# A two-layer PEER and attention stack on one core: the first two output chunks of three projections taken together, and the first picks turned one or two steps sooner

## The reference, cut to what matters

```python
def conformer_conv(h, w1, b1, ...):
    u = h @ w1 + b1                       # 1024 -> 2048: "conv_in"
    a, g = jnp.split(u, 2, axis=-1)
    u = a * jax.nn.sigmoid(g)
    ...
def peer(h, wq, sk1, sk2, u_tab, v_tab):  # once in each of the two layers
    q = (xc @ wq).reshape(PEER_CHUNK, PEER_HEADS, 2, PEER_HALF)   # 1024 -> 2048: "peer_query"
    s1 = jnp.einsum('chd,kd->chk', q[:, :, 0], sk1)
    s2 = jnp.einsum('chd,kd->chk', q[:, :, 1], sk2)
    v1, i1 = lax.top_k(s1, PEER_TOPK); v2, i2 = lax.top_k(s2, PEER_TOPK)
    ...                                   # the 16 best pairs of keys, softmax over their scores
    act = jax.nn.gelu(jnp.einsum('cd,chkd->chk', xc, u), approximate=False)
    return jnp.einsum('chk,chkd->cd', gate * act, v)
```

## Time and profile before

| | us |
|---|---|
| median of 3 runs | 2810.82 (2805.54 to 2812.44) |
| the profiled execution, its own time | 2802.38 |
| its span | 2800.6 |
| TensorE matmul busy | 2706.8 (97%) |
| VectorE busy | 2033.5 (73%) |
| ScalarE busy | 1510.7 (54%) |
| GpSimd busy | 615.6 (22%) |

### The profile page before, as it was taken

The page is one execution under the profiler, slowest core; times in us unless marked ns, Lnnn a source line. Parts: engine busy times, 40 slices in busy tenths (PEclk is TensorE's granted clock), DMA queues, the critical chain, the costliest instruction groups (busy, mean ns, idle before and its releaser), DMA issues.

```text
span 2800.6 us, 60626 instructions
## 1 busy us (share of the span) xinstructions
PE 2706.8 (97%) x21599; PEld 2607.8 (93%) x21599; DVE 2033.5 (73%) x4480; ACT 1510.7 (54%) x3277; POOL 615.6 (22%) x659
## 2 busy tenths in 40 slices
PE   9999999999999998999999999999998899998998
PEld 8899889999999997889899999999987799987998
DVE  7759988787787865779888777777676665556665
ACT  7453355555555554652455555555545655556554
POOL 1033680021111213125850010010044300022000
PEclk9999999999999999999999999999999999999999
DMA  5055427787887843256347677676643046532564
GB/s 182 7 168 175 128 74 248 228 293 248 266 269 245 291 146 117 64 167 201 99 139 233 223 238 237 224 239 221 188 136 125 21 155 186 180 126 78 159 194 135
DMA packets 153654, 493.92 MB, mean 176 GB/s; under 512 B 18033, under 2 KB 37937, under 8 KB 153489
## 3 DMA queue, kind: packets, MB, share of 16 engines
q1 hardware_dynamic: 137424, 437.67, 48.0%
q0 software_dynamic: 15488, 54.11, 6.8%
q10 hardware_dynamic: 576, 0.03, 0.0%
HBM read 481.62 MB, written 10.13 MB: 176 GB/s over the span
## 4 chain that ended last, share of the span: by engine, by line
PE 87%; DVE 8%; ACT 2%; issue 1%; POOL 1%; DMA 0%; POOLq 0%; DVEq 0%; ACTq 0%
PE banks L841 67%; PE banks L1085 7%; PE banks L1244 2%; PE banks L1106 2%; PE banks L983 2%; DVE meta_row L2343 1%; DVE work L2346 1%; PE banks L879 1%; PE banks L874 1%; POOL x_lo L2841 1%; DVE w_lo L545 1%; ACT w_hi L538 1%; DVE arena L2326 1%; PE banks L1361 0%; DVE att_small L2633 0%
## 5 line engine op out<-in xcount | busy, mean ns | idle before, releaser
L545 DVE TENSOR_TENSOR w_lo<-ring,w_hi 128x512 fp32r<-128x512 f32 x1448 | 1014.0, 704 | 551.2 <-ACT w_hi L538 527.2
L538 ACT ACTIVATE w_hi<-ring 128x512 fp32r<-128x512 f32 x1448 | 908.9, 630 | 756.0 <-PE banks L841 710.2
L841 PE MATMUL banks<-gated_all,w_hi 128*128 128x240 f32 (+1 forms) x5120 | 886.2, 278 | 6.4 <-DVE gated_all L2410 6.4
L841 PE MATMUL banks<-x_hi,w_hi 128*128 128x240 f32 (+2 forms) x3008 | 853.2, 284 | 22.5 <-POOL x_lo L2841 7.2
L841 PE MATMUL banks<-x_lo,w_hi 128*128 128x240 f32 (+2 forms) x3008 | 843.7, 280 | 0.0
L841 PE MATMUL banks<-x_hi,w_lo 128*128 128x240 f32 (+2 forms) x3008 | 839.2, 279 | 0.0
L841 PEld LDWEIGHTS banks<-gated_all,w_hi 128*128 128x128 f32 x5120 | 776.5, 190 | 8.3 <-DVE gated_all L2410 8.3
L841 PE MATMUL banks<-gated_all,w_lo 128*128 128x240 f32 (+1 forms) x2560 | 706.9, 276 | 0.0
L841 PEld LDWEIGHTS banks<-x_hi,w_hi 128*128 128x128 f32 x3008 | 572.6, 190 | 36.0 <-issue 13.9
L841 PEld LDWEIGHTS banks<-x_hi,w_lo 128*128 128x128 f32 x3008 | 574.0, 191 | 0.0
L841 PEld LDWEIGHTS banks<-x_lo,w_hi 128*128 128x128 f32 x3008 | 572.4, 190 | 0.5
(11 more groups left out here) (369 smaller groups left out, 2835.2 us busy)
## 6 DMA issues: line engine op xcount, KB each, us to landing
ring<-in_peer_v SPq DMA_DIRECT2D x256, 512.0 KB, 3.6
ring<-in_peer_u SPq DMA_DIRECT2D x184, 512.0 KB, 4.5
arena<-in_peer_u SPq DMA_DIRECT2D x72, 512.0 KB, 3.7
ring<-in_mlp_up SPq DMA_DIRECT2D x64, 512.0 KB, 3.5
ring<-in_mlp_down SPq DMA_DIRECT2D x64, 512.0 KB, 3.5
ring<-w_peer_query SPq DMA_DIRECT2D x32, 512.0 KB, 3.5
ring<-w_fox_proj SPq DMA_DIRECT2D x24, 512.0 KB, 3.5
ring<-w_nsa_proj SPq DMA_DIRECT2D x20, 512.0 KB, 3.5
```

The source lines that it names most:

```text
L538: act.activation(w_hi[:, hn % SPLITS], raw_half(hn), ACT.Copy).then_inc(hi_ready, 1)
L545: dve.tensor_tensor(w_lo[:, hn % SPLITS], raw_half(hn), w_hi[:, hn % SPLITS].bitcast(F32), ALU.subtract)\
L841: mm = pe.matmul(out, w_at(w), x, start=start and j == 0, stop=stop and j == 2, skip_group_check=True)
```

## The change

The first two chunks of conv_in and of both peer_query stages go through a new `project_two`: for each chunk of x it issues the three products of output chunk 0 (bank 0) and then the three of output chunk 1 (bank 1). `half_used` is counted after product (c, i, j) = (3, 0, 2), (7, 0, 2), (7, 1, 0) and (7, 1, 2). In peer_query `presummed` follows both chunks instead of the first. In peer_select `turn(0)` and `store_picks(0)` stand behind `early(22)` in layer 0 and `early(21)` in layer 1 instead of behind `early(23)`, and the exponential of the third tile (layer 0) stands ahead of Gelu 21 on ScalarE instead of behind the last.

```diff
-EXPS_BEFORE = {11: 0, 19: 1}
+EXPS_BEFORE = {11: 0, 19: 1, 21: 2}
+FIRST_TURN = (EARLY_FIRST - 2, EARLY_FIRST - 3)
...
+            def project_two(n, bank, tokens, x_run=None, parts=None, s={}):
+
+                tk_ = moved_slice(tokens) if tokens <= SEQ else x_slice(T0, s)
+                for c in range(NC):
+                    half, c4 = divmod(c, 4)
+                    if x_run is not None:
+                        pe.wait_ge(x_lo_ready, NC * x_run + c + 1)
...
+                    for i in range(2):
+                        if c4 == 0:
+                            pe.wait_ge(lo_ready, 2 * (n + i) + half + 1)
+                        for j, (w, x) in enumerate(((w_hi, x_hi), (w_hi, x_lo), (w_lo, x_hi))):
+                            mm = pe.matmul(banks[:, bank + i, 0:tokens], w[:, half_of(n + i, half), c4 * P:(c4 + 1) * P], x[:, c, tk_],
+                                           start=c == 0 and j == 0, stop=c == NC - 1 and j == 2, skip_group_check=True)
+                            if (c, i, j) in ((3, 0, 2), (NC - 1, 0, 2), (NC - 1, 1, 0), (NC - 1, 1, 2)):
+                                mm.then_inc(half_used, 1)
...
             def conv_in(s):
-                for m in range(16):
+                project_two(s["n0"], 0, T0, x_run=0, s=s)
+                for m in range(2, 16):
...
-                    project(s["n0"] + m, m % 4, T0, x_run=0 if m == 0 else None, s=s)
+                    project(s["n0"] + m, m % 4, T0, s=s)
...
-                    project(s["n0"] + m, m % 4, s["tokens"], x_run=s["x0"] - 2 if m == 0 else None,
-                            beside=spread_in_middle if m == 2 else None)
                     if m == 0:
+                        project_two(s["n0"], 0, s["tokens"], x_run=s["x0"] - 2)
                         presummed(added, s["tokens"])
+                    elif m >= 2:
+                        project(s["n0"] + m, m % 4, s["tokens"], beside=spread_in_middle if m == 2 else None)
...
-                turn(0)
+                    if k == FIRST_TURN[s["layer"]]:
+                        turn(0)
...
                 for k in range(EARLY_FIRST):
-                    if k in EXPS_BEFORE:
+                    if EXPS_BEFORE.get(k, len(tiles)) < len(tiles):
                         exps(EXPS_BEFORE[k])
                     early(k)
+                    if k == FIRST_TURN[s["layer"]]:
+                        store_picks(0)
...
-                if len(tiles) > NT:
-                    exps(NT)
-                store_picks(0)
```

More of the change, by code:

```diff
@@ L859, in project @@
                     mm.then_inc(half_used, 1)
+            def project_two(n, bank, tokens, x_run=None, parts=None, s={}):
[4 more added lines that the diff above has]
+                        pe.wait_ge(x_lo_ready, NC * x_run + c + 1)
+                    if parts is not None:
+                        pe.wait_ge(parts[0], parts[1] + c + 1)
+                    for i in range(2):
[6 more added lines that the diff above has]
+                                mm.then_inc(half_used, 1)
             by_scale = iter([(2, 0), (2, 16), (2, 32), (2, 48), (4, 0), (4, 16), (4, 32), (4, 48)] * 2)
```

## The result

| | median, us | range, us | runs |
|---|---|---|---|
| before | 2805.54 | 2798.24 to 2812.44 | 7 |
| after | 2791.06 | 2784.76 to 2797.41 | 7 |

The ratio is 0.995, 95% interval 0.9932 to 0.9968: faster by 14.5 us, where 3.6 was forecast. The profiled execution of the changed kernel took 2788.46 us with a span of 2786.6; the one of before had 2802.38 and 2800.6. The difference of the spans, 14.0 us, has to be found in the traces.

The account below looks back on a forecast made before the run. TensorE was taken to bound the kernel (87% of the span). The terms, -1.1 + 1.76 + 1.45 - 3.19 - 2.0 - 1.55 + 1.0, summed to -3.6 us, giving 2807.2 us from the median; range 2800 to 2813.

Parts of the forecast that it names:

- How the numbers follow: Section of the prediction that turned its sum and run scatter into chances: faster by over 0.3% 0.15, within 0.78, slower 0.07.
- conv_in, -1.1: conv_in: products fill TensorE's waits for x, so chunk 4 starts sooner; -1.1 us, ends -0.45 and -1.35.
- +1.76 and +1.45: peer_query, layers 0 and 1: the later sum makes TensorE wait for half 4 at chunk 2; us lost per layer.
- +1.0 for the clock: peer_query, both layers: the new idle may drop TensorE's clock; +1.0 us, ends 0 and 3.2.
- turn(0), -3.19 - 2.0 - 1.55: turn(0): layer 0 loses 3.19 us of idle and 2.0 of low clock (ends 0 and -3.0), layer 1 1.55 idle.
- (a): Rival, peer_query: the later sum costs nothing; 2803 us, chance 0.08.
- (b): Rival, peer_query: the new idle drops the clock in both layers, 3.0 us each; 2814 us, chance 0.12.
- (c): Rival, turn(0): the picks are late and TensorE waits inside the turn; 2811 us, chance 0.08.
- (d): Rival, the paired chunks: changing bank every three products slows 144 products, 17 us; 2824 us, chance 0.03.

Follow-up runs that it names:

- the repeat: The changed kernel run once more, nothing edited, beside the kernel before: 2788.52 us against 2794.25, ratio 0.9978.
- split_first: The whole change, with ScalarE's root in peer_query taken behind the split of the halves instead of ahead of it: 2787.39 us, ratio 0.9964 to before.
- query_only: The kernel before with only the two peer_query stages starting with two output chunks together: 2799.86 us, ratio 1.0024 to before.
- turn_only: The kernel before with only the earlier turn(0), its exponential and stored picks: 2787.06 us, ratio 0.9979 to before.
- redraw: The changed kernel plus one unread 16-column identity matmul at the end of each dense loop iteration: 2796.89 us, ratio 1.0001 to before.
- redraw_again: The changed kernel with the identity matmul at the end of each dense iteration, measured a second time: 2798.33 us.
- before_redraw: The kernel before with the same identity matmul at the end of each dense iteration: 2802.14 us.
- wide_loop: split_first with TensorE's dense loop unrolled four times and the identity matmul once in each such iteration: 2790.52 us, ratio 0.9981 to before.
- in_two: The changed kernel with the last product of each dense iteration issued in two column parts: 2793.76 us, ratio 0.9995 to before.

## Why the prediction was wrong in size and right in its parts

**What failed.** The step is the sum taken off before's own execution, with the scatter that "How the numbers follow" gave it: "The median of a few runs scatters by some 3 us". A term for the stages that the edit doesn't touch is missing, that is, it was put at nothing without a reason. The sum took every product of the unedited stages at an unchanged cost. I had read 360 products in 40 us, in one stretch that ran at the shorter spacing, and never set a second stretch beside it; 757 to 980 us of the same trace would have shown 1970 products, where the shorter spacing makes 1993. In before's execution the longer one cost 8366 x 0.00133 = 11 us in the 240-column stretches, and it costs 1462 x 0.0045 = 6.6 us in each MLP stage that has it. No rival had this, and the range from 2800 on couldn't hold 2791.06: 12 runs of one kernel without added matmuls lie 14 to 26 us apart. The first comparison exaggerates the change: the edit is worth -4.7 us with the spacing nearly held, -4.8 by the counted spans, -5.7 by the medians of the repeat.

**conv_in, -1.1.** The convolution starts at 67.10 before and 65.89 after: -1.21. Chunks 0 and 1 ended at 23.0 (22.8 forecast), chunk 4 started at 30.11 (29.97) behind a wait of 0.87 (1.25). No drop of the clock fell on it here. In the traces of all kernels the time from conv_in's first product to the convolution is 52.0 us in three of the five with the old order (52.4 and 53.8 in the others), 50.8 in six with the new one at full clock, and 51.4 to 51.6 in the six where the clock fell to 0.5 in it. So both ends of the term, -1.35 and -0.45, are about right.

**peer_query, +1.76 and +1.45, and +1.0 for the clock.** Layer 0: the wait is 1.73, `w_lo` at 170.26 as the step described, and the clock did fall behind it; from the start of the stage to chunk 15 it takes 3.17 us longer, so the clock had 1.4, one of the term's 1.6. Such a drop behind the new wait is there in three of the seven traces with this part (1.5 us each), and in none of the seven in layer 1; the term of +1.0 for both layers is 0.6 on average. Layer 1: from the first product to chunk 2 it was 1203.83 - 1196.60 = 7.23 before and 1195.95 - 1187.29 = 8.66 after, +1.43. split_first confirms the named cause. Forecast for both layers 4.2, in this trace 3.17 + 1.43 = 4.6, and 5.6 by the runs of query_only.

**turn(0), -3.19 - 2.0 - 1.55.** Both waits are gone, no picks were late, and the groups of layer 0 run at full clock. Peer_select of layer 0 became 5.94 us shorter (5.19 forecast), and that is partly luck: the drop of the clock was there at its largest in this execution of before. From the last product of peer_query to group 0 it takes 89.92 us in all five traces with the old turn and 86.57 in all twelve with the new, -3.35. But from group 0 to the dense stage it takes 104.34, 102.71, 103.02, 101.81 and 101.81 us in the five, and 101.45 to 101.88 in the twelve: the drop costs 2.5, 0.9, 1.2, 0 and 0 us, drawn anew in each execution, 0.9 in the mean where I took 2.0. In layer 1 the stage from chunk 15 of peer_query (1245.98 before, 1238.19 after) to the first `gated_all` product (1439.54, 1429.35) became 2.4 shorter instead of 1.55, and across the other traces it is 2.2 to 2.4. turn_only: -7.2 by the medians against -6.7.

**The parts together.** Taken from the edited stages of all 17 traces, where the spacing of the dense stages plays no part, the means are -1.3 (conv_in), +1.6 and +1.6 (the waits, compared at like clock), +0.6 (clock), -3.35 and -0.9 (turn, layer 0) and -2.3 (layer 1): an estimate of -4.1 us, near the forecast's -3.6 and inside the interval of -7.2 to -2.1. So the sum of the edit's own terms was right; single terms were off by up to 1.1 us and partly cancelled.

**The rivals.** (a) The later sum does cost, until split_first hides it. (b) In the changed kernel's first trace a drop followed in one layer of two, for 1.4 and not 3.0. (c) The picks were in time. (d) `project_two` changes the bank every three products and its 48 products took 7.67 us in layer 0, where the clock was 0.80 in the mean, and 48 in 5.56 us in layer 1, 116 ns each: no slowing of that kind.

**What stays open.** What in an interruption decides for one spacing is not known. Over nine traced executions with the dense loops as they were, 39 of 63 long stretches had the shorter one; behind an added short matmul inside the running stream it was 224 of 227 (redraw and redraw_again, before_redraw, wide_loop, in_two), but behind the kernel's own eight of `sum_gathered` 8 of 27. Nor is it shown why all seven runs of before in the first comparison (2798.24 to 2812.44) lay so high: beside the later kernels its medians were 2794.25, 2796.84, 2796.91 and 2796.71. The one traced execution among them had the longer spacing in four of its five 240-column stretches; the other six have no trace.

## What to carry to other kernels

A kernel that TensorE bounds can differ from itself by 20 us of 2800 with not one instruction changed: before an edit gets the credit, count products per window in stretches that it doesn't touch, in both traces. A comparison with seven runs a side may then still be off by twice the effect; the same kernel again, beside before on the same chip, is the cheapest experiment there is. For an edit of a few stages, the lengths of these stages in several traces tell more than the whole span does: the turn's 3.35 us came out the same to 0.01 us in 17 traces. And when work is moved earlier or later, read whose stream it stands in: here a square root in front of two splits cost 1.6 to 1.7 us in each layer, and swapping them cost nothing.

## What the runs showed of the hardware that was not expected

- TensorE issues one and the same stream of weight load and matmul at one of two exact spacings, at a granted clock of 1.00: 112.0 or 113.3 ns at 240 columns, 113.3 or 117.8 ns at 256. It changed only where the stream was interrupted. The Trainium skill, "TensorE: Matmul & The Clock Gate", section "Back-to-back issue gap", says that the spacing in such a stream is set by load and matmul together, and gives one figure for a column count; the traces here show two.
- A single matmul of 16 columns added inside the stream was followed by the shorter spacing in 224 of 227 pieces, for 0.11 us (part of a product) or 0.225 us (the identity, 108 records for 54). Eight in a row, as the kernel has them between its loops, were followed by it in 8 of 27.
- Behind the same 3.2 us of idle TensorE the granted clock differed from one execution to the next: of five traces with the old turn in layer 0, it was 0.50, 0.72 and 0.67 over the next 5.2 us in three and 1.00 in two, worth 0 to 2.5 us.
- With TensorE's loop of 192 products unrolled four times, a stall of 2.7 to 3.3 us without an instruction came behind the first 768 products of one loop, once in each of the two traces.
